# Compressed-block attention inside the gate products, f32 pairs in the mixers, one more weight slot

## The reference

```python
def mixer_layer(h, ...):
    proj = jnp.einsum('bsd,dc->bsc', h, w_in)
    qa, ka, va, qi, ki, wi, qb, kvb, gb, gate_a, gate_b = jnp.split(proj, SPLIT_POINTS, axis=-1)
...
    o_a = dsa_attention(qa, ka, va, qi, ki, wi)          # indexer picks 128 keys, 8 heads of 64
...
    o_b = nsa_attention(qb, rope(qb, positions), k_cmp, v_cmp, k_slc, v_slc, k_win, v_win, nsa_gates, ...)
    merged = jax.nn.sigmoid(gate_a) * (o_a @ w_br_a) + jax.nn.sigmoid(gate_b) * (o_b @ w_br_b)
    return merged @ w_out

def compress_tokens(kv, pe, w1, w2):                     # 31 blocks of 32 tokens, step 16
    blocks = kv[:, idx] + pe[:, None, :]
    z = blocks.transpose(0, 1, 3, 2, 4).reshape(bsz, n_cmp, hk, CMP_LEN * dh)
    return jax.nn.silu(z @ w1) @ w2
# in nsa_attention: the part that the change moves
        s = jnp.einsum('btkgd,bnkd->btkgn', qn, kc) * scale
        p_cmp = masked_softmax(s, m_cmp)
        o_cmp = jnp.einsum('btkgn,bnkd->btkgd', p_cmp, vc)
```

## Time and profile before

| | us |
| --- | --- |
| median of 3 runs | 2139.77 (2138.37 to 2140.61) |
| the profiled execution, its own time | 2146.05 |
| span in that profile | 2144.8 |
| PE busy | 1879.2 (88%) |
| DVE busy | 1014.5 (47%) |
| ACT busy | 782.6 (36%) |
| POOL busy | 381.0 (18%) |

### The profile page before, as it was taken

How to read it: one execution, slowest core, us unless ns; L and a number is a source line. 1 busy time by engine, 2 the same in 40 slices (tenths; PEclk the granted TensorE clock), 3 DMA queues, 4 the chain that set the end, 5 groups by cost and what they waited for, 6 DMA issues and landing times.

```text
span 2144.8 us, 26954 instructions
## 1 busy us (share of the span) xinstructions
PE 1879.2 (88%) x10524; PEld 1502.3 (70%) x10524; DVE 1014.5 (47%) x1990; ACT 782.6 (36%) x1447; POOL 381.0 (18%) x427
## 2 busy tenths in 40 slices
PE   6979969898798771699889999999899989999997
PEld 5868747677454440578778888787787778888785
DVE  4448666564230105487744433233687554433234
ACT  3232246411243322456534323212666443332211
POOL 0024035300122214024101211000124001110001
PEclk9989979998799996799899999999999899999998
DMA  4333300255899993111033333232211033333231
GB/s 144 88 101 89 118 1 2 79 194 214 322 387 395 397 384 135 39 50 60 21 98 109 98 98 99 81 97 88 69 60 50 20 98 118 99 98 99 89 99 49
DMA packets 134887, 264.46 MB, mean 123 GB/s; under 512 B 11616, under 2 KB 92128, under 8 KB 122464
## 3 DMA queue, kind: packets, MB, share of 16 engines
q1 hardware_dynamic: 116320, 228.35, 31.0%
q10 hardware_dynamic: 13312, 25.90, 3.5%
q0 software_dynamic: 5120, 8.40, 1.2%
HBM read 254.22 MB, written 16.78 MB: 126 GB/s over the span
## 4 chain that ended last, share of the span: by engine, by line
PE 53%; DMA 8%; DVE 7%; ACT 4%; issue 2%; POOL 1%; PEld 1%; PEldq 0%; ACTq 0%; POOLq 0%; DVEq 0%; SPq 0%
PE b L500 15%; PE b L501 14%; PE b L502 14%; DMA m<-in_w_gate_up 6%; PE b L1940 3%; ACT m L613 2%; DMA m<-in_w_down 1%; PE b L2465 1%; PE b L1965 1%; PE b L2451 1%; DVE m L2661 1%; PE b L2485 1%; PE b L2486 1%; DVE m L486 1%; PE b L2487 1%
## 5 line engine op out<-in xcount | busy, mean ns | idle before, releaser
L500 PE MATMUL b<-m,m 128*128 128x512 f32 (+3 forms) x2060 | 787.8, 382 | 80.4 <-DVE m L486 32.2
L501 PE MATMUL b<-m,m 128*128 128x512 f32 (+3 forms) x2060 | 779.0, 378 | 0.0
L502 PE MATMUL b<-m,m 128*128 128x512 f32 (+3 forms) x2060 | 777.7, 378 | 0.0
L486 DVE TENSOR_TENSOR m<-m,m 128x1024 fp32r<-128x1024 f32 (+1 forms) x212 | 279.7, 1326 | 520.9 <-ACT m L476 520.7
L500 PEld LDWEIGHTS b<-m,m 128*128 128x128 f32 x2060 | 396.7, 193 | 155.1 <-issue 33.6
L502 PEld LDWEIGHTS b<-m,m 128*128 128x128 f32 x2060 | 396.7, 193 | 68.7
L501 PEld LDWEIGHTS b<-m,m 128*128 128x128 f32 x2060 | 397.5, 193 | 65.5
L476 ACT ACTIVATE m<-m 128x1024 fp32r<-128x1024 f32 (+1 forms) x236 | 245.7, 1048 | 534.9 <-PE b L502 489.6
L1940 PE MATMUL b<-m,m 128*64 128x256 f32 x1024 | 126.4, 390 | 29.2 <-DMA m<-in_w_gate_up 27.5
L2910 POOL TENSOR_TENSOR m<-m,m 128x512 fp32r<-128x512 f32 x44 | 71.1, 1637 | 422.1 <-ACT m L2856 422.1
L1940 PEld LDWEIGHTS b<-m,m 128*64 128x64 f32 x1024 | 73.6, 139 | 80.6 <-issue 39.8
(11 more groups left out here) (338 smaller groups left out, 2082.4 us busy)
## 6 DMA issues: line engine op xcount, KB each, us to landing
m<-in_w_gate_up SPq DMA_DIRECT2D x64, 1024.0 KB
...
```

The lines of the kernel that those rows point to most:

```text
L486: e.tensor_tensor(flat(wlo[HX[i]], i), flat(raw[RX[i][0]], i), fr(flat(whi[HX[i]], i)), ALU.subtract).then_inc(sem("w_lo"), 1)
L500: e.matmul(out, xh, yh, start=start, stop=False, skip_group_check=True)
L501: e.matmul(out, xh, yl, start=False, stop=False, skip_group_check=True)
L502: return e.matmul(out, xl, yh, start=False, stop=stop, skip_group_check=True)
```

## The change

1. The stage cmp and both its meetings go. Its queries, scores and turn become pieces after gate units 4, 5, 6 and 9 on PE; the v half of the compressor moves from units 3 to 5 to units 10, 12 and 13; the first two `att_turn` follow units 14 and 15, into banks 2 and 3. Evictions of these pieces go to ACT, the position adds, masks and all ropes to POOL, and the softmax of the blocks stays with DVE at units 7 and 8. The wait for the gates' stores moves to `scalar_merge`.
2. `hi_to` and `lo_to` lose their `min(…, 20)`: the first gate chunks are split during the projections.
3. The last tile's scaling goes from DVE to POOL with a semaphore of its own, and the three broadcast loads go from the router to the end of the experts' ACT code.
4. A sixteenth pair slot, (30, 31), is fourth in the list; it waits for w_out's product and lies where gF, gL and bL lie.
5. In the mixers, turned P and V stay f32 in one copy: head 0 of a pair by ACT, head 1 by DVE, V by ACT alone. `tensor_values` becomes eight f32 matmuls of 128x64 by 128x256, the two heads in the two column halves. P has four buffers in place of two pairs.

```diff
-TAIL, GATED, RING, MERGED = 4, 10, 16, 22
-PAIRS = [(4, 5), (6, 7), (8, 9), (10, 11), (12, 13), (14, 15), (0, 1), (2, 3), (16, 17), (18, 19), (20, 21), (22, 23), (24, 25), (26, 27), (28, 29)]
+TAIL, GATED, RING, MERGED, GAINS = 4, 10, 16, 22, 30
+PAIRS = [(4, 5), (6, 7), (8, 9), (30, 31), (10, 11), (12, 13), (14, 15), (0, 1), (2, 3), (16, 17), (18, 19), (20, 21), (22, 23), (24, 25), (26, 27), (28, 29)]
...
-        raw2 += [M.f(2, 1024) for _ in range(3)] + late2[3:7]
+        raw2 += [M.f(2, 1024) for _ in range(3)] + late2[3:7] + [gains]
...
-                elif cells[0] >= RING:
+                elif RING <= cells[0] < GAINS:
                     e.wait_ge(*at("w_used", CH["up0"]))
-                elif cells[0] >= GATED:
+                elif GATED <= cells[0] < RING:
...
+        def tensor_queries(e, pr):
+            if pr >= 2:
+                e.wait_ge(*at("cq_n", pr - 1))
+            else:
+                e.wait_ge(*at("cp_x", 2 * pr + 2))
+            for t in range(NT):
+                m = e.transpose(bank[pr % 2][:, t * P:t * P + P], PJ[:, t, QB + P * pr:QB + P * pr + P], ident)
+            m.then_inc(sem("cq_tr"), 1)
+
+        def scalar_queries(e, pr):
+            e.wait_ge(*at("cq_tr", pr + 1))
...
+            e.activation(QN[pr % 2], bank[pr % 2][:, :], ACT.Copy, scale=-0.125).then_inc(sem("cq_n"), 1)
...
+        def tensor_block_scores(e, pr):
+            e.wait_ge(*at("cq_n", pr + 1))
+            e.wait_ge(*at("cp_k", 4))
+            for t in range(NT):
+                c = 256 * (t % 2) + 64 * pr
+                m = e.matmul(bank[2 + t // 2][:, c:c + 64], QN[pr % 2][:, t * P:t * P + P], kcT[:, pr // 2, :],
+                             start=True, stop=True, skip_group_check=True)
+            m.then_inc(sem("cq_s"), 1)
...
+        def tensor_block_turn(e):
+            e.wait_ge(*at("cv", 10))
+            e.wait_ge(*at("cq_n", 4))
+            for kvh in range(2):
+                for t in range(NT):
+                    m = e.transpose(bank[kvh][:, t * P:t * P + P], SC[:, t, 4 * kvh:4 * kvh + 4, :].rearrange("p h n -> p (h n)"), ident)
+                m.then_inc(sem("cp2"), 1)
...
+        def vector_block_scores(e):
...
+            for t in range(NT):
+                bv = bank[2 + t // 2][:, 256 * (t % 2):256 * (t % 2) + 256].rearrange("p (h n) -> p h n", h=8)[:, :, 0:31]
+                cm = CMv[:, t, 0:31].unsqueeze(1).broadcast_to([P, 8, 31])
+                c.inc(e.tensor_tensor(SC[:, t, :, 0:31], bv, cm, ALU.add))
+            c.wait()
+            c.inc(e.tensor_reduce(cf(0), SCf, AX, ALU.min))
+            c.wait()
+            c.inc(e.tensor_tensor(SCf, SCf, cf(0).unsqueeze(2).broadcast_to([P, 32, 31]), ALU.subtract))
...
                 def after_feat(e, s, fp=fp):
-                    if 2 * fp + s < 6:
-                        tensor_compress(e, 2 * fp + s)
+                    u = 2 * fp + s
+                    if u in (0, 10):
+                        tensor_blocks(e, u // 10)
+                    elif u in (2, 12):
+                        tensor_hidden(e, u // 10)
+                    elif u in (3, 13):
+                        tensor_second(e, u // 10)
+                    elif u == 4:
+                        tensor_queries(e, 0)
+                        tensor_queries(e, 1)
+                    elif u == 5:
+                        for pr in (0, 1):
+                            tensor_block_scores(e, pr)
+                            tensor_queries(e, pr + 2)
+                    elif u == 6:
+                        tensor_block_scores(e, 2)
+                        tensor_block_scores(e, 3)
+                    elif u == 9:
+                        tensor_block_turn(e)
+                    elif u in (14, 15):
+                        att_turn(e, u - 14)
...
-                hi_to(e, min(u + HL, 20))
+                hi_to(e, u + HL)
...
-            e.activation(GNS, PJ[:, :, GB:GB + 24], ACT.Sigmoid).then_inc(sem("gns"), 1)
-            meet(e)
-            for i in range(4):
-                e.wait_ge(*at(f"gs{i}", 64))
+                if u in (0, 10):
+                    scalar_blocks(e, u // 10)
+                elif u == 1:
+                    proj_landed(e, 5)
+                    e.activation(GNS, PJ[:, :, GB:GB + 24], ACT.Sigmoid).then_inc(sem("gns"), 1)
+                elif u in (2, 12):
+                    scalar_hidden(e, u // 10)
+                elif u in (3, 13):
+                    scalar_second(e, u // 10)
+                elif u in (4, 5):
+                    scalar_queries(e, 2 * u - 8)
+                    scalar_queries(e, 2 * u - 7)
+                elif u == 7:
+                    scalar_block_exp(e)
+                elif u == 9:
+                    scalar_block_turn(e)
...
-                lo_to(e, min(u + HL, 20))
...
-                if u < 6:
-                    vector_compress(e, u)
                 vector_topk(e, u)
+                if u == 7:
+                    vector_block_scores(e)
+                elif u == 8:
+                    vector_block_weights(e)
             vector_topk(e, 16)
-            meet(e)
-            for i in range(4):
-                e.wait_ge(*at(f"gs{i}", 64))
...
             gpsimd_compress(e, 0)
+            gpsimd_block_masks(e)
+            gpsimd_blocks(e, 0)
+            gpsimd_compress(e, 1)
             c = Chain(e, *at("rp"))
-            rope(e, c, PJ[:, :, QA:QA + 256], 4, 32, NCS, NSN, TG)
-            gpsimd_compress(e, 1)
-            for col, nh, cs, sn in ((QA + 256, 4, NCS, NSN), (KA, 1, CS, SN), (KVB + 256, 2, CS, SN), (KVB + 512, 2, CS, SN)):
+            for col, nh, cs, sn in ((QA, 4, NCS, NSN), (QA + 256, 4, NCS, NSN), (KA, 1, CS, SN), (KVB + 256, 2, CS, SN), (KVB + 512, 2, CS, SN)):
...
             e.wait_ge(*at("cq_tr", 4))
-            r = Chain(e, *at("rq_g"))
-            rope(e, r, PJ[:, :, QB + 384:QB + 512], 2, 32, NCS, NSN, TG)
-            meet(e)
-
+            for col in (QB, QB + 256):
+                rope(e, c, PJ[:, :, col:col + 256], 4, 32, NCS, NSN, TG)
+            e.wait_ge(*at("cp_tr", 3))
+            att_dup(e, 0)
+            gpsimd_blocks(e, 1)
+            c.wait()
...
+        TBK, OBK, PBK = [4, 5], 6, [2, 3] + 11 * [7]
...
-            for p in range(3):
-                att_turn(e, p)
...
             c0 = CH["branch"]
+            gates_stored(e)
...
-            e.tensor_scalar(XN2[t], XN2[t], st2[:, t:t + 1], None, ALU.mult).then_inc(sem("n2_xn"), 1)
...
-            e.dma_start(gF, io["norm_final"].partition_broadcast(P)).then_inc(sem("gF"), 16)
-            e.dma_start(gL, io["ln_in_g_2"].partition_broadcast(P)).then_inc(sem("gL"), 16)
-            e.dma_start(bL, io["ln_in_b_2"].partition_broadcast(P)).then_inc(sem("gL"), 16)
...
-            normed(e, 3)
...
+            normed(e, 3)
...
+            e.wait_ge(*at("w_used", CH["mix0"]))
+            e.dma_start(gF, io["norm_final"].partition_broadcast(P)).then_inc(sem("gF"), 16)
+            e.dma_start(gL, io["ln_in_g_2"].partition_broadcast(P)).then_inc(sem("gL"), 16)
+            e.dma_start(bL, io["ln_in_b_2"].partition_broadcast(P)).then_inc(sem("gL"), 16)
...
-            e.wait_ge(*at("meet", 24))
+            e.wait_ge(*at("meet", 16))
...
-                for tt in range(2):
-                    m = e.activation(v_dst(0, j, tt), v_src(o, tt), ACT.Copy)
+                m = e.activation(VV[:, 2 * (n % 2):2 * (n % 2) + 2, 4 * (n // 2):4 * (n // 2) + 4, :],
...
-            for hh in range(2):
-                ph, pl = PT2[hh]
-                sl = slice(64 * hh, 64 * hh + 128)
-                for kt in range(NT):
-                    vh, vl = VV[0][:, kt, p, sl], VV[1][:, kt, p, sl]
-                    e.matmul(o, vh, ph[:, kt, :], start=hh == 0 and kt == 0, stop=False, skip_group_check=True)
-                    e.matmul(o, vl, ph[:, kt, :], start=False, stop=False, skip_group_check=True)
-                    m = e.matmul(o, vh, pl[:, kt, :], start=False, stop=hh == 1 and kt == 3, skip_group_check=True)
+            for kt in range(NT):
+                for hh in range(2):
+                    m = e.matmul(o[64 * hh:64 * hh + 64, :], VV[:, kt, 2 * p + hh, :], PT2[2 * hh + m_ % 2][:, kt, :], start=kt == 0, stop=kt == 3, skip_group_check=True)
...
         def scalar_turn_p(e, l, k):
-            n = NST * l + k
-            for hh in range(2):
-                e.wait_ge(*at("m_t", 2 * n + hh + 1))
-                if k >= 2:
-                    e.wait_ge(*at("m_pv", 8 * l + k // 2))
-                e.activation(PT2[hh][0][:, :, P * (k % 2):P * (k % 2) + P], bank[4 + hh][:, :].rearrange("p (k n) -> p k n", n=P), ACT.Copy).then_inc(sem("m_h"), 1)
+            e.wait_ge(*at("m_t", 2 * (NST * l + k) + 1))
+            turned_free(e, l, k)
+            e.activation(*turned(k, 0), ACT.Copy).then_inc(sem("m_h"), 1)
...
         def vector_turn_p(e, l, k):
-            n = NST * l + k
-            for hh in range(2):
```

(6 more changed lines are left out.)

359 lines of the change are left out of this document (161 added, 198 removed).

## The result

The changed kernel took 2071.22 us (median of 4, 2061.19 to 2073.48) beside 2140.19 before (median of 4): ratio 0.9657, 95% interval 0.9633 to 0.9681. The profiled execution took 2073.48, 72.6 less than the 2146.05 of before. The page has PE busy for 1849.8 us, 29 less, so over half of the gain is idle time of PE that went. Single executions of the changed kernel lie up to 12 us apart.

What follows compares the result with a forecast made beforehand. PE was taken to bound the kernel (busy 1879 of 2145 us), with DMA bounding the experts. Parts A to H summed to −69.4 us, taking the median from 2139.77 to 2070.4, stated as 2070; range 2058 to 2086.

Steps and rivals of the forecast that it cites:

- Part A: Start of the gates: early halves remove PE's 10.56 us stall and the half clock after it; −12.7 us.
- Part B: Hidden product in the gates: PE's wait for DVE's position adds goes, as POOL does them; −2.7 us.
- Part C: Gates: PE takes up 32 transposes, sixteen score matmuls and 0.3 us on each of eight pieces; +10.6 us.
- Part D: Stage cmp: the chain from last gate matmul to first attention score goes, except short remainders; −34.0 us.
- Part E: Router's last tile: earlier scaling and store, gather 3.3 us sooner and up to 1 us shorter; −4 us, bounds −1.5 to −6.
- Part F: Sixteenth slot: one more 1.05 MB load before the experts' DMA-bound stream; −2.7 us, other bound 0.
- Part G: Mixers: cheaper product with V, no V wait, fewer DVE copies in the tail; −24.4 us in two layers.
- Part H: First block's end: ACT issues three broadcasts before the meeting, mostly beside POOL's last scatter; +0.5 us.
- Heads that don't overlap: Mixers: column halves exclude each other, so sixteen records take 3.8 us; 2101 at worst, 2085 if half overlaps; chance 0.1.
- Late helpers in the gates: Gates: PE waits 5 us twice for POOL's queue, half clock following; A to D worth 15 less, 2085; chance 0.13.
- The slow clock: Gates: inserted pieces with waits hold PE at 1.2 GHz through the sixteen units; 2148 us, slower than before; chance 0.02.
- The router's part and the slot as nothing: Router and experts: the routing table, not the store, starts the gather, and PE ends the experts; 2077 us; chance 0.1.

Runs made afterwards that it cites:

- the run with held loads: Changed kernel with broadcasts behind the output loads, block weights ahead of top-k, and SP's last two loads before the experts held until POOL scaled the last tile: 2062.37 us.
- the run with heads in turn: Changed kernel with the product with V running all four key tiles of head 0, then all of head 1, instead of alternating: 2082.52 us, ratio 0.9705.

## Why the prediction was right, step by step

2070 was forecast and 2071.22 came, but the terms were not that good; several errors cancel.

**Part A** (−12.7): 10.56 + 2.48 = 13.0 in the traces. Undoing it alone gave 10.5 by the medians and 11.8 at the place.

**Part B** (−2.7) was mis-sized: the wait also had half clock behind it. In the kernel before:

```profile
168.71 5.71 PE L970 MATMUL b<-m,m 128*128 128x63 f32 x32 [2.67 <-DVE m L1007]
174.18 0.77 PE L500 MATMUL b<-m,m 128*128 128x512 f32 x1
174.75 0.63 PE L501 MATMUL b<-m,m 128*128 128x512 f32 x1
```

From start to start this product took 174.18 − 168.71 = 5.47 us; the second one, at full clock, took 3.49. The seven matmuls behind it took 3.03 in place of some 1.67. With the wait that is 2.8 + 2.0 + 1.4, so B was worth −6.2.

**Part C** (+10.6) had nearly the right sum from wrong terms. From the first gate matmul to the end of the last it took 106.06 before (151.57 to 257.63) and 108.64 after (142.31 to 250.95), +2.6. Taking out A's half clock (2.5) and B's 6.2 leaves +11.2. Of this, 3.1 is the new wait before the block turn and 1.4 the half clock behind it, so the inserted work costs 6.7. The steps from start to start say nearly the same: 28 transposes 2.75 (the block turn at full clock), 32 records of scores 3.36, and 0.09 more for the first matmul behind each of five pieces. The step that failed is the price of a piece. I divided printed lengths (1.04 for eight transposes), but the step from one start to the next is what counts, 0.10:

```profile
182.21 1.00 PE L1056 MATMUL b<-m,m 128*128 128x64 f32 x8
183.04 0.60 PE L1042 MATMUL b<-m,m 128*128 128x128 f32 x4
183.41 0.48 PE L507 MATMUL b<-m,m 128*128 128x512 f32 x1
```

And the fill of 0.3 on each of eight pieces (2.5) was 0.09 on five; the 0.80 of the earlier trace rows, which I read as a fill, is just eight steps of 0.10. These errors of some 4 us were made up by the new wait, which the prediction didn't have. That the sum came out is luck.

What I missed is that top-k stands ahead of the block weights on DVE: it began at 202.62 in the trace after, the weights behind it at 205.58 and they ended at 210.2, while PE had finished unit 9 at 207.3. POOL's ropes, which I feared, were done at 208.9 and kept nobody waiting.

**Part D** (−34.0): 35.37 before, 1.22 now, −34.15. A to D sum to −42.1 from the end of the projections, against −38.8; nearly all of the difference is B's.

**Part E** (−4): −4.8 in the traces, with another split than forecast. Counted from the router's last logits, the gather begins 2.3 us sooner (forecast 3.3) and takes 2.5 less (forecast up to 1). From the last logits to the first expert matmul, undoing the early scaling alone costs 2.7, and putting the broadcasts back 2.7 (by the medians 3.5 and nothing), so the two overlap a little. What I didn't foresee is the store: with the early issue it took 13.60 us. Here the page "DMA: Bandwidth & Descriptors" of the Trainium skill (Queues, rings and completion order) says that each engine takes turns between queues; the prediction read −6 from it. The runs agree that order of issue doesn't rule (the run with held loads), but not with the gain: the store took 12 to 14 us whenever it was issued early, and 8.34 when it came late, so of 7 us of earlier issue 2.7 reached the gather.

**Part F** (−2.7): −0.6 to −1.8 by taking the slot away. The step that failed is the term "1.05 MB is 2.7 us": one more load ahead is not a whole load's time less behind. The table's 2.6 agrees by chance, for it holds the broadcasts too: with them back in the router this stretch took 1.6 longer. Where the rest of the load's time goes was not settled.

**Part G** (−24.4): −23.2 to the end of the span, 27.0 by its undoing. Its terms in layer 0: from the first score to a small product near the end of the projections (L2362 at 1016.87 before, L2413 at 960.55 after) −7.0, forecast −8.8; the tail from there −4.5, forecast −3.4. In the tail the transposes still wait for DVE, 2.8 us in both layers where it was 6.0; the prediction's sign "no transposes wait for DVE in the tail" did not come.

The product itself is 1.95 us as forecast, but its edges cost something. Before:

```profile
954.06 1.09 PE L2465 MATMUL b<-m,m 128*128 128x128 f32 x8
954.91 0.36 PE L2485 MATMUL b<-m,m 128*128 128x256 f32 x1
...
957.86 0.40 PE L500 MATMUL b<-m,m 128*128 128x512 f32 x1
958.09 0.40 PE L501 MATMUL b<-m,m 128*128 128x512 f32 x1
```

and after:

```profile
900.84 1.09 PE L2506 MATMUL b<-m,m 128*128 128x128 f32 x8
901.87 1.95 PE L2524 MATMUL b<-m,m 128*64 128x256 f32 x16
903.74 0.50 PE L507 MATMUL b<-m,m 128*128 128x512 f32 x1
904.08 0.40 PE L508 MATMUL b<-m,m 128*128 128x512 f32 x1
```

The eight transposes up to the product take 1.03 where they took 0.85, and the first matmul behind it 0.34 where it took 0.23. From the transposes to the second matmul behind the product it is 3.24 in place of 4.03: −0.8 each, not −1.0. The page "TensorEngine Tiling (Array Packing)" of the Trainium skill (Key Properties) says that a change of mode drains TensorE. The 0.18 at the entry and 0.11 at the exit may be that or include it; a first matmul behind plain transposes also takes 0.31 to 0.32, and no run separates the two.

What fell short is V's wait, "3.3 + 0.5" to nothing. In the profiled execution DVE's next job has it now:

```profile
881.64 3.40 DVE L641 TENSOR_TENSOR m<-m,m 128x1024 f32<-128x1024 f32 x1
884.96 0.74 DVE L2453 SCALAR_TENSOR_TENSOR m<-b,m,m 128x512 fp32r<-128x512 f32 x1
```

```profile
881.59 2.36 POOL L2739 TENSOR_TENSOR m<-m,m 128x1024 fp32r<-128x1024 f32 x1 [4.32 <-PE b L2492]
```

```profile
L507 PE MATMUL b<-m,m 128*128 128x512 f32 x65 | 26.4, 406 | 2.2 <-DVE m L2453 2.2
```

An addition of two such tiles takes 1.22 us elsewhere and 3.40 here, where POOL's operation began 0.05 us before it. V's subtraction came behind it before, Q's (L2453) does now, and PE waits 2.2 where it waited 3.3. The repeat of the same program has the other order in layer 0, and there it is POOL that takes longer:

```profile
883.88 1.23 DVE L641 TENSOR_TENSOR m<-m,m 128x1024 f32<-128x1024 f32 x1
```

```profile
883.89 3.46 POOL L2739 TENSOR_TENSOR m<-m,m 128x1024 fp32r<-128x1024 f32 x1 [4.38 <-PE b L2492]
```

So the two operations exclude each other, and whichever begins first goes unhindered. When DVE is first, PE has no wait for Q at all, and the stretch from the first score to L2413 takes 99.8 us in place of 102.0. That is −9.1 against the 108.94 of before, close to the forecast −8.8. Over the eleven traces with the new mixers, two layers each, POOL was first in eleven of 22 layers: both in the first profile, one in its repeat. Before the change, and with the mixers as before, POOL was 0.1 us ahead in every layer, and V's wait of 3.3 stood behind the same addition, which took 3.3 us. This race, 2.2 us a layer, is a part of why executions of one program differ.

**Part H** (+0.5): +2.65, and +2.3 to +4 over eight traces. "most of it lies beside POOL's last scatter" was the error: beside it is in its way.

**Rivals.** Heads that don't overlap: the run with heads in turn shows what it would have been, 11.8 us. Late helpers in the gates: not POOL, but DVE, by 4.5 us in the first profile. The slow clock: 0.98 to 1.00 through the gates. The router's part and the slot as nothing: the router's part was 4.8, and the store still came last, since the gather began 1.0 after its landing.
